# RWKV head sums on a Trainium2 core: 64x64 blocks of ones in all four quarters of TensorE, with variance and bonus side by side

## The reference, cut to what matters

```python
def _rwkv_prep(p, mu, w0, w2, a0, a2, g2, k_k, k_a):
    ...
    kk = heads(kf * k_k)
    kk = kk / jnp.maximum(jnp.sqrt(jnp.sum(kk * kk, axis=-1, keepdims=True)), 1e-12)   # norm of the key
    ...

def _rwkv_out(y, r, k_dir, v, g, ln_w, ln_b, r_k):
    mean = jnp.mean(y, axis=-1, keepdims=True)
    var = jnp.mean(jnp.square(y - mean), axis=-1, keepdims=True)                        # variance of the output
    yn = ((y - mean) * lax.rsqrt(var + RWKV_GN_EPS)).reshape(b, t, MIX_WIDTH) * ln_w + ln_b
    k_b = 0.5 * (k_dir[0] + k_dir[1])
    bonus = (jnp.sum(r * k_b * r_k, axis=-1, keepdims=True) * v).reshape(b, t, MIX_WIDTH)   # bonus
    return ((yn + bonus) * g).astype(g.dtype)
```

## Time and profile before

| | us |
|---|---|
| median of 3 runs | 3804.96 |
| lowest and highest | 3797.29, 3809.39 |
| the profiled execution, device time | 3807.08 |
| its span in the trace | 3805.3 |
| PE busy in the span | 3467.8 (91%) |
| DVE, ACT, POOL busy | 1608.9 (42%), 1046.8 (28%), 676.1 (18%) |
| the eight RWKV units of the first layer, in the trace | about 870 to 1470 |
| those of the second layer | about 2765 to 3320 |

### The profile page before, as it was taken

The page is one execution under the profiler, slowest core; times in us unless marked ns, Lnnn a source line. Parts: engine busy times, 40 slices in busy tenths (PEclk is TensorE's granted clock), DMA queues, the critical chain, the costliest instruction groups (busy, mean ns, idle before and its releaser), DMA issues. The chain is left out here.

```text
span 3805.3 us, 92574 instructions
## 1 busy us (share of the span) xinstructions
PE 3467.8 (91%) x41720; PEld 1975.8 (52%) x41720; DVE 1608.9 (42%) x2844; ACT 1046.8 (28%) x1829; POOL 676.1 (18%) x583
## 2 busy tenths in 40 slices
PE   7899999999999979989999598998999998789997
PEld 3454445545666665443332345656666666674333
DVE  3574704646666562120000356824166766421111
ACT  2211004304555451021111321104145555211001
POOL 0141201303334240010000002113023333200000
PEclk9999999999999999989999799999999999999998
DMA  5104523431101010339998211833311110068996
GB/s 198 66 1 143 177 66 89 166 91 32 30 22 28 19 48 24 122 155 421 406 388 351 101 47 49 265 109 86 94 30 30 33 30 28 25 239 332 424 424 272
DMA packets 238877, 538.58 MB, mean 142 GB/s; under 512 B 49264, under 2 KB 157056, under 8 KB 205584
## 3 DMA queue, kind: packets, MB, share of 16 engines
q1 hardware_dynamic: 219424, 463.87, 33.1%
q0 software_dynamic: 19056, 68.69, 5.1%
HBM read 514.64 MB, written 17.87 MB: 140 GB/s over the span
## 5 line engine op out<-in xcount | busy, mean ns | idle before, releaser
L1260 PE MATMUL banks<-sb_h,sb_ring 128*128 128x512 f32 (+1 forms) x1344 | 474.8, 512 | 10.1 <-DMA sb_ring<-w_branch 6.5
L1754 PEld LDWEIGHTS banks<-inv 64*64 64x64 f32 x15104 | 299.3, 137 | 188.4 <-issue 186.1
L1754 PE MATMUL banks<-inv 64*64 64x64 f32 x15104 | 336.3, 224 | 51.9 <-issue 19.0
L1260 PEld LDWEIGHTS banks<-sb_h,sb_ring 128*128 128x128 f32 x1344 | 254.3, 190 | 223.8 <-issue 196.1
L1763 PE MATMUL banks<-sb_h,sb_ring 128*128 128x512 f32 (+1 forms) x672 | 329.0, 597 | 7.0 <-DMA sb_ring<-w_in 4.0
L780 PE MATMUL banks<-sb_h,sb_ring 128*128 128x512 f32 x512 | 231.2, 609 | 19.4 <-SPq L244 19.4
L3189 DVE TENSOR_TENSOR hrow<-hrow,banks 128x256 f32<-128x256 f32 x36 | 15.1, 421 | 374.2 <-ACT hrow L3223 374.2
L780 PEld LDWEIGHTS banks<-sb_h,sb_ring 128*128 128x128 f32 x512 | 99.3, 196 | 138.5 <-issue 117.8
L1260 PE MATMUL banks<-sb_branch,sb_ring 128*128 128x512 f32 (+1 forms) x512 | 170.9, 487 | 0.0
L3039 PE MATMUL banks<-gu,xs 128*64 128x512 f32 x768 | 168.6, 594 | 2.2 <-DMA gu<-gu_pairs 1.6
L2439 DVE COPY inv<-banks 128x512 f32<-128x512 f32 x144 | 98.8, 691 | 163.3 <-PE banks L1754 162.5
(11 more groups left out here) (419 smaller groups left out, 5673.2 us busy)
## 6 DMA issues: line engine op xcount, KB each, us to landing
gu<-gu_pairs SPq DMA_DIRECT2D x64, 1536.0 KB, 15.9
gu<-gu_tiles SPq DMA_DIRECT2D x57, 1024.0 KB, 9.5
sb_ring<-w_in SPq DMA_DIRECT2D x24, 2048.0 KB, 9.0
sb_ring<-gu_tiles SPq DMA_DIRECT2D x39, 1024.0 KB, 9.8
vtok<-w_mod POOLq DMA_DIRECT2D x64, 512.0 KB, 5.3
sb_ring<-down_pairs SPq DMA_DIRECT2D x32, 1024.0 KB, 14.1
sb_ring<-w_in SPq DMA_DIRECT2D x26, 1024.0 KB, 5.3
sb_ring<-down_tiles SPq DMA_DIRECT2D x25, 1024.0 KB, 8.8
```

The source lines that it names most:

```text
L1260: mm = nc.tensor.matmul(out, left(kt), right(kt), start=kt == 0, stop=kt == KT - 1)
L1754: m = mm(k.bank[bank][H[to], at:at + w], left, right, start=start, stop=True, skip_group_check=True)
```

## The change

The 128x128 `headones` goes from the three sums. `head_sum` takes its place: a matmul with a 64x64 block of ones, from one head's 64 partitions to 64 partitions of a bank, either the same ones or the other head's (`swapped`). The four combinations of source half and target half are the four quarters of TensorE's array.

- **Norm**: four matmuls of 256 columns. The first 256 tokens go to bank 0 in place, the other 256 to bank 1 with the heads swapped. DVE's `bound_norm` becomes three operations: one over 128 partitions and 256 columns, two over 64 partitions and 256 columns, which swap the heads back. Since bank 1 is used now, PE waits for ACT's copies of `inverse(b, 3)` ahead of the norm.
- **Variance and bonus**: two matmuls each, issued in turn (variance head 0, bonus head 0, variance head 1, bonus head 1). The variance stays in place, the bonus swaps the heads, so that together they take all four quarters. For that the variance moves behind both parts of `gram_pair(c, 1, ...)`, beside the bonus. In the second layer the bonus now covers 256 columns where it covered 512. DVE's `bonus` becomes two operations over 64 partitions in place of one over 128.
- One product of stage 1 moves from bank 3 to bank 5, so that the wait for the bonus's reader (`s.bvd`) moves from stage (1, 2) to stage (2, 1).

```diff
@@ STAGES
-     [(0, "q0", "XT", "XT", 0, "add", 1), (1, "X", "XT", "XT", 1, "copy", 3)]],
+     [(0, "q0", "XT", "XT", 0, "add", 1), (1, "X", "XT", "XT", 1, "copy", 5)]],
@@ TensorE
+            def head_sum(out, a, h, swapped, done):
+                mm(out[H[h ^ swapped]], ones64[H[h]], a[H[h]], start=True, stop=True, skip_group_check=True).then_inc(done, 1)
+
-            def gate_and_norm(c):
+            def gate_and_norm(c, b=None):
...
                 pe.wait_ge(s.kksq, c(1, 1))
-                mm(k.bank[NORM_BANK], const(k, "headones"), tmp, start=True, stop=True).then_inc(s.kkn, 1)
+                if b:
+                    hold(s.ev_a, b(N_EV_A, AFTER[3][1]))
+                for h in range(2):
+                    for swapped in range(2):
+                        head_sum(k.bank[NORM_BANKS[swapped]][:, 0:LC], tmp[:, LC * swapped:LC * swapped + LC], h, swapped, s.kkn)
...
-            def bonus(b):
-                hold(s.bonus_in, b(1, 1))
-                hold(s.nevac, b(6, 6))
-                mm(k.bank[BONUS_BANK], const(k, "headones"), ks[:], start=True, stop=True).then_inc(s.bonus_d, 1)
+            def bonus(h):
+                head_sum(k.bank[BONUS_BANK][:, t0:], ks[:, t0:], h, 1, s.bonus_d)
...
                     if (g, i) == (1, 2):
                         hold(s.plus, b(2, 1))
-                        hold(s.bvd, b(1, 1))
+                    if (g, i) == (2, 1):
+                        hold(s.bvd, b(2, 2))
...
                     gram_turned(c)
+                    for part in range(2):
+                        gram_pair(c, 1, part, [] if part else [(s.gevac, c(6, 2)), (s.gevac, c(6, 2))], s.gdone)
+                    hold(s.bonus_in, c(1, 1))
+                    hold(s.nevac, c(6, 6))
                     if b:
                         hold(s.rawin, r_kept)
-                        variance(b)
-                    for part in range(2):
-                        gram_pair(c, 1, part, [] if part else [(s.gevac, c(6, 2)), (s.gevac, c(6, 2))], s.gdone)
-                    bonus(c)
-
-            def variance(b):
-                pe.wait_ge(s.sq, b(1, 1))
-                mm(k.bank[SUM_BANK][:, 0:n], const(k, "headones"), yq[:, t0:], start=True, stop=True).then_inc(s.var_d, 1)
+                        hold(s.sq, b(1, 1))
+                    for h in range(2):
+                        if b:
+                            variance(h)
+                        bonus(h)
+
+            def variance(h):
+                head_sum(k.bank[SUM_BANK][:, 0:n], yq[:, t0:], h, 0, s.var_d)
@@ VectorE
             def bound_norm(f, c):
-                v.wait_ge(s.kkn, c(1, 1))
-                ts(tmp, k.bank[NORM_BANK], 1e-24, 65536.0, ALU.max, ALU.mult).then_inc(s.normin, 1)
+                v.wait_ge(s.kkn, c(4, 4))
+                ts(tmp[:, 0:LC], k.bank[NORM_BANKS[0]][:, 0:LC], 1e-24, 65536.0, ALU.max, ALU.mult).then_inc(s.normin, 1)
+                for h in range(2):
+                    ts(tmp[H[h], LC:], k.bank[NORM_BANKS[1]][H[1 - h], 0:LC], 1e-24, 65536.0, ALU.max, ALU.mult).then_inc(s.normin, 1)
...
-                stt(bv[:, t0:], k.bank[BONUS_BANK][:, t0:], 0.5, vv[:, t0:], ALU.mult, ALU.mult).then_inc(s.bvd, 1)
+                for h in range(2):
+                    stt(bv[H[h], t0:], k.bank[BONUS_BANK][H[1 - h], t0:], 0.5, vv[H[h], t0:], ALU.mult, ALU.mult).then_inc(s.bvd, 1)
```

More of the change, by code:

```diff
@@ L1689, in rwkv_heads @@
         spread = lambda ap, m=NC: one(ap).to_broadcast([P, m, 64])
-        eye64, centre64 = const(k, "eye64"), parts.centre
+        eye64, ones64, centre64 = const(k, "eye64"), const(k, "ones")[:, 0:64], parts.centre
         p1 = lambda j: pc[:, j:j + 1]
@@ L1697, in rwkv_heads @@
         GRAM_BANKS, TURNED_BANKS, OTHER_BANK = ((1, 2), (5, 6)), (0, 4), 3
-        RATE_BANKS, GATE_BANK, NORM_BANK, GTV_BANKS, P2_BANKS = (4, 0), 4, 0, (4, 0), ((1, 2), (3, 6))
+        RATE_BANKS, GATE_BANK, NORM_BANKS, GTV_BANKS, P2_BANKS = (4, 0), 4, (0, 1), (4, 0), ((1, 2), (3, 6))
         MOVE_BANKS, N_BANKS, CHAIN_BANKS, Y_BANK, SUM_BANK = ((0, 1), (3, 4)), (2, 6), (0, 3), 4, 7
@@ L2014, in mix @@
                 if c:
-                    gate_and_norm(c)
+                    gate_and_norm(c, b)
                 inverse(b, 4)
@@ L2019, in mix @@
                     hold(s.gate_in, c(1, 1))
-                    hold(s.normin, c(1, 1))
+                    hold(s.normin, c(3, 3))
                 gram_times_v(b)
@@ L2056, in last_rows_and_merge @@
                 gate(0, range(2))
-                variance(b)
+                pe.wait_ge(s.sq, b(1, 1))
+                for h in range(2):
+                    variance(h)
                 gate(0, range(2, KT))
@@ L2081, in _ @@
             pe.wait_ge(s.gate_in, 1)
-            pe.wait_ge(s.normin, 1)
+            pe.wait_ge(s.normin, 3)
             projection(2, second_w3)
@@ L2124, in inverse_norm @@
             def inverse_norm(c):
-                act.wait_ge(s.normin, c(1, 1))
+                act.wait_ge(s.normin, c(3, 3))
                 ac(tmp, tmp, ACT.Ln).then_inc(s.less, 1)
@@ L2150, in bonus_bias @@
             def bonus_bias(b):
-                act.wait_ge(s.bvd, b(1, 1))
+                act.wait_ge(s.bvd, b(2, 2))
                 ac(bv[:, t0:], bv[:, t0:], ACT.Identity, bias=ln[:, 1:2]).then_inc(s.bvr, 1)
@@ L2188, in root @@
             def root(b):
-                act.wait_ge(s.var_d, b(1, 1))
+                act.wait_ge(s.var_d, b(2, 2))
                 ac(yq[:, t0:], k.bank[SUM_BANK][:, 0:n], ACT.Ln, scale=1.0 / 64, bias=fixed[:, 1:2]).then_inc(s.vlog, 1)
@@ L2413, in bonus @@
             def bonus(m, b):
-                v.wait_ge(s.bonus_d, b(1, 1))
+                v.wait_ge(s.bonus_d, b(2, 2))
                 m.do(nc.vector.tensor_copy(ln[:], pc[:, LNW:LNB + 1]))
-                stt(bv[:, t0:], k.bank[BONUS_BANK][:, t0:], 0.5, vv[:, t0:], ALU.mult, ALU.mult).then_inc(s.bvd, 1)
+                for h in range(2):
+                    stt(bv[H[h], t0:], k.bank[BONUS_BANK][H[1 - h], t0:], 0.5, vv[H[h], t0:], ALU.mult, ALU.mult).then_inc(s.bvd, 1)
                 for z, a, e, w in ((0, 0, 1, 7), (1, 1, 0, 3), (1, 5, 4, 3), (1, 0, 7, 1)):
```

## The result

| | before | after |
|---|---|---|
| median of 9 runs each, us | 3809.17 | 3818.08 |
| lowest and highest | 3797.29, 3818.91 | 3813.38, 3826.68 |
| ratio, 95% interval | | 1.0032 [1.0021, 1.0043] |
| profiled execution and its span | 3807.08, 3805.3 | 3815.18, 3813.3 |
| first stretch, L0 | 591.61 | 597.21 |

The changed kernel is slower by 0.3%, 9 us, where 6 us less were forecast. A **stretch** is from here on the time from a layer's first gate matmul in its RWKV units to the first gate matmul of the merge behind them, both read off PE in order of time. A **standstill** is an idle time of PE that the profile puts down to "issue"; the sums of "issue" count those over 0.15 us. Both are read from one profiled execution of each kernel.

The account below looks back on a forecast made before the run. PE, busy 544 of 600 us in the first layer's window, was taken as nearest the bound, with ACT nearly level in the crossings. Norm -5.6, first layer +1.9, second -2.0 made -5.7 us: 3799 forecast, range 3785 to 3814.

Parts of the forecast that it names:

- What a block of ones costs: Four 64x64 quarters at once take the time of one: 1.06 us at 512 columns, 0.62 at 256.
- Both rivals that let them wait for each other: Row halves take turns in a bank: +9 us, 3814, 7%; quarters overlap only in a chain: 3822, 7%.
- Norm: Norm on PE from 1.02 to 0.62 us, 0.40 less in 14 units: -5.6 us; later `bound_norm` costs nothing.
- if that cover were gone: Behind the norm, without PE work covering the later `bound_norm`: up to 1.0 us a unit.
- DVE's bonus: Two DVE operations for one, +0.69 us in the first layer, just fitting before `inverse(b, 2)`: nothing, or up to 0.1.
- First layer, crossing: Variance leaves a wait, ACT's chain ends later: four crossings +3.2 us, three -0.1, -0.2, -1.0; layer +1.9.
- Second layer: Variance and bonus over 256 columns take 0.62 us where bonus took 1.06: -2 us, between -3.5 and +1.
- between -2 (the standstills stay and ACT has room): Low end of the first layer's sum of +1.9 us; the high end is +6.7, all seven crossings like the first.
- if the standstills end at the same time: Second layer's unfavourable case, standstills ending at the same time whatever precedes them: +1 us.
- the first rival: All of the saved work arrives, in crossings of both layers and norms: 20 us less, 3785; 15%.
- the 'issue' standstills move elsewhere: Rival: every crossing is like the first, 7 x 0.95 us, second layer 0, norms -5.6: +1, 3806; 15%.
- The starting point: Profiled 3807.1 us less 5.7 gives 3801.4; that execution was 2.1 above the runs' median, so 3799.

Follow-up runs that it names:

- six pairs: Changed kernel against before at four placements (0 to 192 increments ahead), and at two with `hold`'s increments left out: stretches 2.5 us longer, "issue" 13.8 more.
- before_fused: Kernel before with the `s.passed` increment left out of `hold` on PE, the wait kept: median 3788.54 us, ratio to before 0.9956 [0.9938, 0.9973].
- the best kernel: Kernel before without `hold`'s increments on PE, with the new norm and a 128x128 bonus over the wanted columns only, variance at its old place: ratio 0.9915 [0.9893, 0.9938].

## Why the prediction was wrong, step by step

- **What a block of ones costs**: right, and a little too dear. Four at 512 columns take 0.88 us, not 1.06. Both rivals that let them wait for each other fell. The Trainium skill's "TensorEngine Tiling (Array Packing)", Gotcha 1, would keep different row tiles out of one bank at a time; here two halves of the rows write bank 7 and two write bank 3, on different partitions of it, and the rows at 1044.98 and 1045.08 show them together.
- **Norm**: right in most units, wrong at both ends of a layer. Behind the gate PE waits 0.15 us more and needs 0.57 less: -0.42 us in nine of the fourteen units, between -0.12 and -0.33 in the others, where -0.40 was forecast. The later `bound_norm` was put at nothing, on the ground that 1.8 us of PE's work cover it. In the last norm of each layer that cover is missing: the products that need it start 0.87 and 1.00 us later, as the forecast's own "if that cover were gone" has it. In each layer's first unit it costs 0.3 us. The sum of the norms is about -3 us, not -5.6. Long standstills follow soon after those two waits in both kernels, so what they cost in the end stays open. DVE's bonus (1.41 us for 0.69) holds nobody up.
- **First layer, crossing**: the waits came as described (1.33 us before the grams; 1.07 us more from `inverse(b, 0)` to `inverse(b, 1)`). In six of the seven crossings that second term was 1.0 to 1.4 us and in one 0.5, where the forecast had four of 0.5 to 1.0. Summed, it is 7.2 us. From the first grams to `inverse(b, 0)` the seven take 5.9 less. Two standstills inside the grams (2.44 and 2.20 us) have gone from there, one of 2.21 us has come in another crossing, and the one in the last has grown by 1.06. That makes +1.3, where +1.9 was forecast, but it is near by luck: crossing by crossing it runs from -2.8 to +2.3 us, moved by borders that the forecast took as fixed.
- **Second layer**: in the crossings `inverse(b, 0)` starts 0.4 to 0.6 us sooner after the sums' start, where 0.44 was forecast; the standstills eat that (six of seven crossings have one of 1.1 to 2.3 us in `inverse(b, 0)` or just behind it, where before the longest was 1.0), and the stretch is 0.8 us longer, not 4.8 shorter.
- **The step that failed** is the one that took the "issue" standstills for fixed in place and length, "between -2 (the standstills stay and ACT has room)" and "if the standstills end at the same time". They were costed as a cover for other work, not as a resource that runs out. They grew by 17.3 us, and what the borders cost, read from start to start, by about 24. The sum without them is +6.4 - 17.3 = -10.9 or +6.4 - 24 = -18; the forecast's was -5.7. By the second figure most of the saved work does arrive, as the first rival said (20 us), and is lost again at the borders. The rival "the 'issue' standstills move elsewhere" had the right name and a price of 7 us, less than half. And the 44 us of "issue" in the trace of before, 4% of the stretches, should have been asked what they wait for before anything else: with 91% busy the rest looked too small to matter.
- **The starting point**: of the 19 us between the forecast of 3799 and the 3818 measured, 4 are the median of the kernel before, which was 3804.96 in the first three runs and 3809.17 in nine.

**What stays open.** That the growth of "issue" belongs to the change is shown by six pairs out of six; by layer it grows in all six second layers, and in the first in four, with two level (-0.9 and +0.3 us). Why it grows is argued: at 2 us for a block's worth of dense products and 2.75 us or more from border to border, time taken out of the few long matmuls is time in which the next block would have come. That the timed pair's +6.4 rather than the average is due to the placement rests on single executions; outside the stretches the two kernels differ by 2 us besides. Between the layers before_fused takes 9.0 us longer than before (1314.6 against 1305.5 from stretch to stretch), so that the median fell by 15 us where the stretches fell by 30; that wasn't followed up.

## What to carry to other kernels

Where a profile shows "issue" among an engine's waits, look at the instruction queue, and at which instruction numbers they fall, before costing anything: if blocks come as fast as they can, a saving in long instructions can be lost again at the borders, and taking out short ones helps (852 of 92,574 gave 0.4%, the best kernel 0.85%). Compare such a change at several placements of the blocks, since the same work differed by 12 us, more than the change is worth, and run one placement twice to see what an execution alone moves (here up to 4 us in a layer). A matmul that lies in a wait should stay there, even where it could be made shorter beside another.

## What the runs showed of the hardware

- PE's instructions come in 16 KB blocks at 3.23 us or more from start to start, about 1 us each to move, and PE goes on 1.2 to 1.8 us after one has landed. Its standstills of over 0.4 us fall on borders of 256 instructions (66 of 66). Dense 64x64 products use a block up in 2.07 us.
- The same instructions, moved by 64 to 192 places, took 1137 to 1150 us; at the same placement a layer repeated within 0.3 to 3.9 us.
- 64 semaphore increments on PE took 9.7 us, 0.15 us each; with 852 instructions fewer, increments behind waits, the two stretches lost 30 us, 18 of them near block borders.
- Four 64x64 matmuls of 512 fp32 columns in the four quarters took 0.88 us together, one 128x128 of as many columns 1.02 to 1.06; over 256 columns 0.49 us (3129.98 to 3130.47 in the changed kernel) against 0.62.
